# A layer norm's shift taken as the mean over six of eight feature tiles instead of four, in a two-block transformer kernel

## The reference

```python
def layer_norm_2(x, g, b):
    mu = jnp.mean(xf, -1, keepdims=True)
    var = jnp.mean(jnp.square(xf - mu), -1, keepdims=True)
    return ((xf - mu) * lax.rsqrt(var + LN_EPS_2) * g + b).astype(x.dtype)
```

## Time and profile before

| what | value |
|---|---|
| time, median of 3 runs | 3029.02 us (3028.34 to 3030.21) |
| the profiled execution's own time | 3032.17 us |
| its span, first to last instruction | 3030.4 us |
| PE busy | 2857.2 us (94%), 16360 instructions |
| DVE busy | 918.2 us (30%) |
| ACT busy | 354.0 us (12%) |
| DMA, mean | 226 GB/s, 684.05 MB |
| mean granted PE clock | 0.990 of 2.4 GHz |

### The profile page before, as it was taken

One profiled execution on the slowest core, in us unless ns is written; L12 is line 12 of the kernel. 1 busy time (PEld: TensorE's weight loads), 2 busy tenths in 40 slices (PEclk: granted clock), 3 DMA queues, 4 the chain that ended last, 5 costly groups with the idle time before them and its releaser, 6 DMA issues.

```text
span 3030.4 us, 39490 instructions
## 1 busy us (share of the span) xinstructions
PE 2857.2 (94%) x16360; PEld 2014.8 (66%) x16360; DVE 918.2 (30%) x1927; ACT 354.0 (12%) x718; POOL 52.8 (2%) x92
## 2 busy tenths in 40 slices
PE   7999999998888889999988888899999999999998
PEld 3554444476565667788744444488788887888887
DVE  1232331352222233432411111179733202333211
ACT  0022220020000002121200000011221001112000
POOL 1000000000000001000000000000000000000000
PEclk9999999999999999999999999999999999999999
DMA  8442245159999993234599999944233443342441
GB/s 333 167 160 108 108 163 218 70 218 421 421 420 421 420 408 114 94 105 136 196 422 420 420 421 421 421 173 153 82 137 112 153 153 125 125 143 101 153 153 42
DMA packets 97805, 684.05 MB, mean 226 GB/s; under 512 B 11632, under 2 KB 12784, under 8 KB 17136
## 3 DMA queue, kind: packets, MB, share of 16 engines
q1 hardware_dynamic: 91632, 660.17, 55.1%
q0 software_dynamic: 6016, 21.50, 2.3%
HBM read 678.22 MB, written 3.41 MB: 225 GB/s over the span
## 4 chain that ended last, share of the span: by engine, by line
PE 74%; DMA 22%; DVE 2%; issue 1%; ACT 1%; SPq 0%; DVEq 0%; ACTq 0%
PE ps L621 29%; DMA ring<-units 22%; PE ps L896 11%; PE ps L1061 6%; PE ps L925 3%; PE ps L1366 2%; PE ps L1200 2%; PE ps L721 1%; PE ps L1076 1%; PE ps L717 1%; PE ps L1017 1%; PE ps L944 1%; PE ps L810 1%; PE ps L831 1%; PE ps L1047 1%
## 5 line engine op out<-in xcount | busy, mean ns | idle before, releaser
L621 PE MATMUL ps<-h,ring 128*128 128x256 f32 (+1 forms) x2176 | 503.7, 394 | 6.6 <-ACT h L1545 6.6
L621 PEld LDWEIGHTS ps<-h,ring 128*128 128x128 f32 x2176 | 414.8, 191 | 93.5 <-issue 39.5
L1076 PE MATMUL ps<-ring,arena 128*32 128x256 f32 x3072 | 382.1, 384 | 54.8 <-DMA ring<-units 51.4
L1061 PE MATMUL ps<-ring,arena 128*64 128x256 f32 x3072 | 350.8, 384 | 58.7 <-DMA ring<-units 55.0
L1076 PEld LDWEIGHTS ps<-ring,arena 128*32 128x32 f32 x3072 | 185.1, 110 | 243.5 <-DMA ring<-units 101.2
L1061 PEld LDWEIGHTS ps<-ring,arena 128*64 128x64 f32 x3072 | 236.6, 138 | 165.7 <-issue 82.4
L896 PE MATMUL ps<-u,ring 128*128 128x512 f32 (+1 forms) x1024 | 339.9, 487 | 0.0
L621 PE MATMUL ps<-arena,ring 128*128 128x256 f32 x1408 | 305.6, 379 | 1.3 <-DVE arena L2693 1.3
L621 PEld LDWEIGHTS ps<-arena,ring 128*128 128x128 f32 x1408 | 267.5, 190 | 38.0 <-DVE arena L2610 1.7
L896 PEld LDWEIGHTS ps<-u,ring 128*128 128x128 f32 x1024 | 193.9, 190 | 134.2 <-issue 120.8
L2323 DVE COPY u<-ps 32x512 f32<-32x512 f32 (+1 forms) x128 | 70.9, 554 | 211.8 <-PE ps L1076 119.1
(11 more groups left out here) (367 smaller groups left out, 2552.9 us busy)
## 6 DMA issues: line engine op xcount, KB each, us to landing
ring<-units SPq DMA_DIRECT2D x624, 1024.0 KB, 13.4
arena<-quarters POOLq DMA_DIRECT2D x32, 256.0 KB, 2.9
h<-tokens SPq DMA_DIRECT2D x1, 2048.0 KB, 24.5
arena<-neighbours POOLq DMA_DIRECT2D x32, 64.0 KB, 4.9
arena<-tokens POOLq DMA_DIRECT2D x1, 2048.0 KB, 9.1
arena<-memory POOLq DMA_DIRECT2D x2, 1024.0 KB, 7.0
con<-constants SPq DMA_DIRECT2D x1, 1712.0 KB, 22.2
early_values<-arena POOLq DMA_DIRECT2D x6, 256.0 KB, 5.0
```

The costliest lines, as they stand in the source:

```text
L621: last = nc.tensor.matmul(ps[:, g + j, 0:n], w[:, kt, j * P:(j + 1) * P], rhs[:, q * KT + kt, 0:n], start=(q == 0 and kt == 0), stop=(q == ...
L1061: last = nc.tensor.matmul(ps[j * slots:(j + 1) * slots, bank, lo:lo + UC], lhsT[:, kt, 0:slots], w[j][:, kt, :], start=(kt == 0), stop=(kt ...
L1076: last = nc.tensor.matmul(ps[j % 4 * slots:(j % 4 + 1) * slots, banks[j // 4], 0:UC], lhsT[:, kt, 0:slots], w[j][:, kt, :], start=(kt == 0 ...
```

## The change

The shift becomes the mean over six tiles, pairs 0 to 2. DVE adds pair 2 first and folds all three pairs; PE sums them in the middle of the fourth projection; the shift is 4/3 of that sum; DVE takes it off three pairs, and only pair 3 gets it ahead of its product. The sum of tiles 4 and 5 falls away, on DVE and on PE. The folding of the squares of pairs 0 to 2 is no longer between the third and the fourth projection but behind `residual(3)` on DVE, and PE sums the folded tile last, behind the squares of pair 3. The square of the rest of the mean goes to a tile of its own.

```diff
 def rest_and_squares(x, sq, rest, n, g):              # PE
-    pe.wait_ge(rest_folded, at(rest_folded))
-    nc.tensor.matmul(ps[:, g, 0:n], mean, rest[:, 0:n], start=True, stop=False)
-    pe.wait_ge(squares_folded, at(squares_folded))
-    nc.tensor.matmul(ps[:, g + 1, 0:n], mean, sq[:, 0, 0:n], start=True, stop=False)
     pe.wait_ge(centred, at(centred, KT // 2))
     for kt in (KT - 2, KT - 1):
-        last = nc.tensor.matmul(ps[:, g, 0:n], mean, x[:, kt, 0:n], start=False, stop=(kt == KT - 1))
+        last = nc.tensor.matmul(ps[:, g, 0:n], mean, x[:, kt, 0:n], start=(kt == KT - 2),
+                                stop=(kt == KT - 1))
     last.then_inc(shift_left, 1)
     pe.wait_ge(squares_ready, at(squares_ready, KT // 2))
     for kt in (KT - 2, KT - 1):
-        last = nc.tensor.matmul(ps[:, g + 1, 0:n], mean, sq[:, kt, 0:n], start=False, stop=(kt == KT - 1))
-    last.then_inc(squares_summed, 1)
+        last = nc.tensor.matmul(ps[:, g + 1, 0:n], mean, sq[:, kt, 0:n], start=(kt == KT - 2), stop=False)
+    pe.wait_ge(squares_folded, at(squares_folded))
+    nc.tensor.matmul(ps[:, g + 1, 0:n], mean, sq[:, 0, 0:n], start=False, stop=True).then_inc(squares_summed, 1)
...
-                middle=(lambda: shift_sum(folded, n, g)) if c == 2 else None)
+                middle=(lambda: shift_sum(folded, n, g)) if c == 3 else None)
...
 def shifted_normalize(...):                            # ACT
-    A(sq[:, KT - 3, 0:n], ps[:, g, 0:n], ACT.Square).then_inc(rest_squared, 1)
+    A(rest[:, 0:n], ps[:, g, 0:n], ACT.Square).then_inc(rest_squared, 1)
...
 def shifted_normalize(...):                            # DVE
     link(v.tensor_tensor(folded[:, :, 0:n], pair[0], pair[1], ALU.add))
+    residual(2)
+    settle()
+    link(v.tensor_tensor(folded[:, :, 0:n], folded[:, :, 0:n], pair[2], ALU.add))
     v.tensor_tensor(folded[:, 0, 0:n], folded[:, 0, 0:n], folded[:, 1, 0:n], ALU.add).then_inc(part_folded, 1)
     dve.wait_ge(shift_summed, at(shift_summed))
-    link(v.tensor_scalar(off, ps[:, g, 0:n], 2.0, None, ALU.mult))
-    for c in range(2):
+    link(v.tensor_scalar(off, ps[:, g, 0:n], 4.0 / 3.0, None, ALU.mult))
+    for c in range(3):
         v.tensor_tensor(pair[c], pair[c], wide(off, [P, 2, n]), ALU.subtract).then_inc(centred, 1)
-    for c in range(2, 4):
-        less_shift(c, wide(off, [P, 2, n]))
+    less_shift(3, wide(off, [P, 2, n]))
     settle()
-    residual(2)
-    settle()
-    v.tensor_tensor(rest[:, 0:n], x[:, 4, 0:n], x[:, 5, 0:n], ALU.add).then_inc(rest_folded, 1)
+    residual(3)
     for c in range(2):
         dve.wait_ge(squares_ready, at(squares_ready, 2 - c))
         link(v.tensor_tensor(sq[:, 0:2, 0:n], sq[:, 0:2, 0:n], sq[:, 2 * c + 2:2 * c + 4, 0:n], ALU.add))
     v.tensor_tensor(sq[:, 0, 0:n], sq[:, 0, 0:n], sq[:, 1, 0:n], ALU.add).then_inc(squares_folded, 1)
     count.skip(squares_ready, 1)
-    residual(3)
```

More of the change, by code:

```diff
@@ L439, in build @@
         shift_summed = sem("shift_summed")
-        rest_folded = sem("third_pair_folded")
         squares_folded = sem("squares_folded")
@@ L1388, in even_mixer @@
                     out_half(c, 0, None if c else lambda kt: pe.wait_ge(conv_ready, kt // 2 + 1),
-                             (lambda: shift_sum(fold, S, g)) if c == 2 else None)
+                             (lambda: shift_sum(fold, S, g)) if c == 3 else None)
                 rest_and_squares(t1, t2, leftover, S, g)
@@ L1528, in normalize, with shifted_normalize @@
                 state["product"] += 1
-            def shifted_normalize(x, sq, n, tiles, gain, shift, eps):
+            def shifted_normalize(x, sq, n, rest, tiles, gain, shift, eps):
                 load_log_exp()
@@ L1630, in layer @@
                 state["product"] += 4
-                shifted_normalize(u, sq1, T, h, V("ln1_g")[:, l * KT:], V("ln1_b")[:, l * KT:], eps1)
+                shifted_normalize(u, sq1, T, gated[:, 1, :], h, V("ln1_g")[:, l * KT:], V("ln1_b")[:, l * KT:], eps1)
                 nc.scalar.preload_act_table_set("exp_and_others")
@@ L1700, in latent_norm @@
             def latent_norm(n):
-                shifted_normalize(t1, t2, S, h, V("ln_g")[:, n * KT:], V("ln_b")[:, n * KT:], eps2)
+                shifted_normalize(t1, t2, S, leftover, h, V("ln_g")[:, n * KT:], V("ln_b")[:, n * KT:], eps2)
             def memory_attention(l):
@@ L1926, in shifted_normalize @@
                 dve.wait_ge(squares_summed, at(squares_summed))
-                v.tensor_tensor(off, ps[:, g + 1, 0:n], sq[:, KT - 3, 0:n], ALU.subtract).then_inc(variances_ready, 1)
+                v.tensor_tensor(off, ps[:, g + 1, 0:n], rest[:, 0:n], ALU.subtract).then_inc(variances_ready, 1)
                 less_rest(0)
@@ L2196, in residual @@
                                                           ALU.mult, ALU.add)
-                    if c >= 2:
+                    if c == 3:
                         last.then_inc(centred, 1)
@@ L2349, in add_product @@
                 pair = t1[:, 2 * c:2 * c + 2, :]
-                if c < 2:
+                if c < 3:
                     v.scalar_tensor_tensor(pair, h[:, 2 * c:2 * c + 2, 0:S], ALPHA, y, ALU.mult, ALU.add)
```

## The result

| | before | after |
|---|---|---|
| median | 3030.80 us | 3036.47 us |
| lowest to highest of 20 runs each | 3028.34 to 3035.01 | 3033.48 to 3039.55 |
| span of the profiled execution | 3030.4 us | 3037.8 us |
| mean granted clock | 0.990 | 0.990 |

The ratio is 1.0019, 95% interval 1.0013 to 1.0025: 5.7 us slower (3.9 to 7.6). The forecast was 3034.1 on a median of 3029.02 that three runs had given; against before, it was +5.1. The change is slower, since the interval leaves out 1, by a size just under the 0.2% (6.1 us) that the prediction took as its bound. The profiled execution of the changed kernel was the slowest of its twenty (3039.55 us), so the 7.4 us between the two spans isn't the size of the change.

What follows compares the result with a forecast made beforehand. PE, 94% busy, was taken to bound the kernel, DVE mattering only where PE waits at eight norms. 7 x 0.6 + 0.86 = 5.1 us on the median 3029.02 gave 3034.1 us; range 3030.8 to 3037.6, the forecast's own 3032.3 to 3036.0.

Steps and rivals of the forecast that it cites:

- The sums in front of pair 3 were filling, not path: At the norms, PE's early sums stood in its wait for pair 3; removing them gains nothing, at most a few hundredths.
- the sums been on the path: Rival, before pair 3: early sums were path, so each norm gets two passes shorter; -3.9 us, 3025.1; chance 0.05.
- The move of the shift costs nothing: Fourth projection: shift's sum half a projection and a half later stalls neither PE nor DVE; cost nothing.
- Two passes behind the squares of pair 3, 0.6 us: Seven norms of 256 columns: PE sums the late fold after pair 3's squares, 0.6 us each, bounds 0.43 to 0.8.
- a product that starts late: Folded tile's sum on PE: fold 0.04 us after pair 3's squares, plus 0.05 for PE starting after DVE.
- The wide norm, 0.86: ln1 norm over 512 columns: fold ends while PE is busy, so it costs just its two passes, 0.86 us.
- The clock rival: Three unfilled norms with work behind: added idling brings further falls to 1.2 GHz; 10.2 us, or 6.8 with one; chance 0.16.
- Filled norms forgive it: Rival: four norms with fill work hide the extra passes, only the other four pay; 2.4 us, 3031.4; chance 0.09.

Runs made afterwards that it cites:

- the emptied kernel: Kernel before without PE's two early sums (tiles 4 and 5, folded squares), their waits kept: 0.9995 (0.9986 to 1.0004), -1.5 us.
- the part alone: Kernel before, shift still over four tiles, with only the squares' fold moved behind residual(3) and its sum last on PE: 1.0015, 4.5 us slower.
- the removal: Changed kernel without PE's sum of the folded squares and its wait, DVE's fold kept: 0.9998 to the kernel before, -0.6 us.
- the doubling: Changed kernel with PE's sum of the folded squares made twice: 1.0023 to the kernel before, 7.0 us slower.

## Why the prediction was right, and where it was off

- *The sums in front of pair 3 were filling, not path.* Shown by the emptied kernel, whose narrow tails are 2.91 and not shorter than 2.84. Its time, -1.5 us (-4.2 to 1.2), says the same: had the sums been on the path, the four passes taken away would give 7 x 0.86 + 1.72 = 7.7 us. The 3.9 us in what was expected of that run is wrong, since it still counts the two passes that only the changed kernel adds.
- *The move of the shift costs nothing.* Shown in the timeline: 1.25 us to spare before the sum (1.3 forecast), 0.50 before pair 3 (0.44).
- *Two passes behind the squares of pair 3, 0.6 us.* Shown by the tails of the part alone, the removal and the doubling; the times agree, less sharply. The size was a little high: 0.49 to 0.56. The forecast put 0.09 on a product that starts late. In the norm behind the first memory attention it started 0.88 us after the squares of pair 3, whose four passes take 0.86, and in the even mixer's with no delay at all (2247.33 to 2248.19). The sum is then 4.7 us and not 5.1.
- *The wide norm, 0.86.* The two passes are 0.87 in the kernel with the late fold alone. In the changed kernel 1.8 us of clock came on top, in its profile, in a norm with fill work, where I had the clock down as safe. The clock rival had its place wrong (the three norms without fill work, where the falls were there already and no more came) and was right that a further fall could appear. There is one fall fewer elsewhere: behind the first norm after an MLP the granted clock was 0.50 and 0.58 in two stretches of 3.2 us in a row before, and 0.59 and then 1.00 in the changed kernel. Falls come and go like this over the whole span: an estimate from stretches of 1 us gives about 64 us at 1.2 GHz before and 60 after, and the mean granted clock is 0.990 in both. So how much of the measured 5.7 us the clock makes on average isn't settled: 4.7 lies well inside the interval, and so does 6.5 (4.7 + 1.8).
- *The closeness of 5.1 to 5.7 is in part luck.* The passes were sized 0.4 us too high, and the wide norm's fall wasn't in the sum.
- *Filled norms forgive it.* No: the even mixer's and the odd mixer's norms show the longer tail too, and the norms behind them come 0.56 and 0.62 us later, counted from there. What the two filled `ln1` norms pass on was not measured apart.
- *The median.* Three runs gave 3029.02, twenty 3030.80. The absolute forecast was 2.4 us low, of which 1.8 is this.

## What to carry to other kernels

Work that an engine did while it waited for something else cost no time here, and behind that something all of it was path; ask of each moved instruction what it stood beside. The two sums deleted from the wait gained nothing. Find the wait that ends last, here for a pair of tiles of which the first was long ready, and split that. The chain of waits alone would have misled here; the idle time in brackets told it.

## What was not expected of the hardware

Six idle-time matmuls in each of four norms, 2.75 us of PE work each time whose result nobody reads, made the kernel 3.9 us faster; the granted clock stayed at 1.00 where it had averaged 0.57 over 3.2 us. The Trainium skill ("TensorE: Matmul & The Clock Gate", "What's actually happening") has it that the throttled clock is the default and activity releases it; the trace agrees. And waits of nearly equal length in the same norm were followed by 1.2 GHz in four kernels (1.91 to 1.98 us) and by 2.4 GHz in another (1.84 us).
